# A fused two-layer encoder trunk: the first feed-forward's last down product in two passes, a Sqrt and a reciprocal for the norm behind it, and GpSimd on four rows of the final norm

## The chip, the cores and the metric

The kernel runs on one core of a Trainium2 chip. The metric is the device time of one execution in microseconds (us), the median of three timed runs. The profile comes from one further execution. TensorE (PE) does matrix products into PSUM, VectorE (DVE), ScalarE (ACT) and GpSimd (POOL) work element by element, SyncE (SP) starts DMAs. Each engine has its own instruction stream; they meet at semaphores.

## What is computed

Two streams of frames (1024 prompt frames and 64 sample frames, D = 1024) pass through two layers that share all weights:

```
for layer in range(2):
    x = x + mixer(rmsnorm(x, norm_mix[layer]))       # layer 0: RG-LRU, layer 1: RWKV-7
    x = x + conv_ffn(rmsnorm(x, norm_ffn[layer]))    # D_FF = 3072
y = rmsnorm(x, norm_final)

rmsnorm(x, g)  = x * rsqrt(mean(x*x, -1) + 1e-6) * g
conv_ffn(h)    : u = causal_dwconv(h @ w_up); g, val = split(u); (gelu(g) * val) @ w_down
rwkv7 (start)  : prev = shift(h); xx = prev - h; x_j = h + xx*mu_j for six j; then r, k, v, w, a, g from x_j
```

Recurrent states of each mixer and convolution are outputs too.

## The kernel before

**Layout.** Activations are transposed: `X` is 8 rows (row k holds channels 128k to 128k+127 on the 128 partitions) of 1092 columns (1024 prompt frames, a gap of 4, 64 sample frames). A row is cut into three column blocks of 364. `WIDE` is the first two blocks (728 columns), `LAST` the third (364). A product is in three parts (high by high, high by low, low by high) of values split in two, so each 128x128 weight block costs three matmuls per column block. `ACC[0]` is PSUM banks 0 to 2, `ACC[1]` banks 3 to 5; product m goes to `ACC[m % 2]`, signals `acc_ready`, and TensorE starts product m + 2 only when product m has been taken (`taken0`, `taken1`). Weight tiles come in by DMA to `RAW`, ScalarE makes the high part `WH` (`w_hi`), GpSimd the low part `WL` (`w_lo`).

**A feed-forward** has 12 steps of four up products and eight down products; each down product d adds to row d of `X`. VectorE takes it (`X[d] += ACC`).

**The norm behind the first feed-forward** (`norm`, L520 on ScalarE, L1321 on TensorE, `take_all` on VectorE). The last eight down products have full width (18 matmuls each). VectorE takes row d, ScalarE squares it into a scratch row, VectorE adds the squares into `T[:, 3]`. When seven squares have been added, TensorE sums over partitions with a matrix of ones (`ONES`), plain fp32 matmuls: three blocks of `T[:, 3]`, then three of the last square. ScalarE turns the sum into the factor, Ln and then Exp with scale -0.5, with a table load between. VectorE then forms row k of the RWKV input, `HF[k] = X[k] * mix1[k] * factor`, ScalarE copies it to `HS[k]`, VectorE subtracts for the low part, and TensorE begins the first two RWKV products (L1444), 36 matmuls per k. Beside the down products GpSimd prepares those products' weights: from `RAW` it forms the shift weights (L1147, L1149), waits for ScalarE's copy (`sh_hi`), and makes low parts of them (`sh_lo`) and of two weight tiles (`w_lo`); TensorE waits for both `sh_lo` and both `w_lo` before it begins L1444.

**The kernel's end** (`final_down`, `final_rows`, `final_square`, `final_root`). Here the last down product already has two passes: eight products over WIDE (12 matmuls each), then eight over LAST (6 each). After the fourth LAST product TensorE sums the WIDE squares; after the eighth, the LAST ones in two matmuls. VectorE computes `X * final * factor` row by row, eight WIDE rows (three LAST adds fall between them) and eight LAST rows, and SyncE sends each row out, all WIDE rows first.

The wait that orders VectorE's own stream: each of its instructions waits for its predecessor's semaphore (`own`).

Of the kernel before, what the change touches and what calls it, by code (L numbers as in the profile page):

```python
# [138 lines left out]
M_PROJ = M_N2 + 1  # L139
# [28 lines left out]
def build(nc, io):  # L168
    ctx = ExitStack()
    with ctx:  # L170
# [86 lines left out]
        def sum_parts(m):  # L257
# [8 lines left out]
            w_hi w_lo acc_ready taken0 taken1 pads vprep absv hist kept tap conv gelu squared primed summed normed root_ln rstd y_dve  # L266
# [12 lines left out]

        ONES, MG = CO[:, 0:P], CO[:, C_MG:C_MG + P]  # L280
# [48 lines left out]
        def _(sp):  # L329
# [156 lines left out]
            for cols in (WIDE, LAST):  # L486
                for k in range(KT):
                    sp.wait_ge(*t.next("y_dve"))
                    sp.dma_start(io["yT"][k][:, cols], X[:, k, cols]).then_inc(*t.made(f"dma_y{k % 2}"))
# [6 lines left out]
        def _(act):  # L496
# [23 lines left out]
            def norm(m, source, n=None, weights=None):  # L520

                nonlocal sums
                for k in range(KT):
                    if weights == "two" and k == KT // 2:
                        w_hi(n, m - KT // 2)
                    source(k)
                    if k >= 3:
                        act.wait_ge(*t.at("summed", sums + k - 2))
                    run(T[:, 3 if k == 0 else 4 + k % 2, 0:COLS], X[:, k, :], ACT.Square, "squared")
                sums += KT - 2  # L530
                run(DV[:, 13, 0:1], CO[:, 0:1], ACT.Ln, "primed")
                if weights == "both":
                    w_hi(n, 0)
                if weights in ("both", "two"):
                    w_hi(n + 1, m)
                evacuate(m, row3(T[:, 2, 0:COLS]), ACT.Ln, bias=RMS_EPS, scale=1.0 / D)
                run(T[:, 2, 0:COLS], T[:, 2, 0:COLS], ACT.Exp, "rstd", scale=-0.5)
# [162 lines left out]
            plus = added(m - KT)  # L700

            def added_and_shift(k):
                if k in (1, 3):
                    act.wait_ge(*t.next("mu_w"))
                    run(TR[:, 6 + k // 2, 0:D], T[:, k // 2, 0:D], ACT.Copy, "sh_hi")
                plus(k)

            norm(m, added_and_shift, n, "two")
# [332 lines left out]
            def final_square(m, k, cols, base):  # L1041

                act.wait_ge(*t.at(f"taken{m % 2}", m // 2 + 1))
                if k >= 3:
                    act.wait_ge(*t.at("summed", base + k - 2))
                run(T[:, 3 if k == 0 else 4 + k % 2, cols], X[:, k, cols], ACT.Square, "squared")

            def final_root(sums_at, out):

                act.wait_ge(*t.next("normed"))  # L1050
                run(out, sums_at, ACT.Ln, "root_ln", bias=RMS_EPS, scale=1.0 / D)
                run(out, out, ACT.Exp, "rstd", scale=-0.5)

            m -= KT
            for k in range(KT):
                final_square(m + k, k, WIDE, sums)
# [13 lines left out]
        def _(pool):  # L1070
# [206 lines left out]
            ffn()  # L1277


        @block.tensor  # L1280
        def _(pe):
# [38 lines left out]

            def norm(m):  # L1321

                if m >= 2:
                    pe.wait_ge(*t.at(f"taken{m % 2}", m // 2))
                pe.wait_ge(*t.next("summed", KT - 2))
                for j in range(CH):
                    pe.matmul(ACC[m % 2][:, j, :], ONES, T[:, 3, j * CW:(j + 1) * CW], start=True, stop=False)
                pe.wait_ge(*t.next("squared", KT))
                for j in range(CH):
                    mm = pe.matmul(ACC[m % 2][:, j, :], ONES, T[:, 5, j * CW:(j + 1) * CW], start=False, stop=True)  # L1330
                mm.then_inc(*t.made("acc_ready"))
# [51 lines left out]
            def final_down(m, n):  # L1383
# [21 lines left out]
                pe.wait_ge(*t.next("summed", KT - 2))  # L1405
# [4 lines left out]
            def ffn(m, n, final=False):  # L1410
# [336 lines left out]
            ffn(m, n, final=True)  # L1747
# [3 lines left out]
        def _(dve):  # L1751
# [72 lines left out]
            def take_all(m, last, bias=False, first=0):  # L1824
# [5 lines left out]
                if last:  # L1830
                    t.n["squared"] += 1
# [603 lines left out]
```

## Time and profile before

| | |
|---|---|
| timed runs | 3153.45 us median (3153.28 to 3154.48) |
| profiled execution, its own time | 3144.15 us |
| span of the profiled execution | 3142.3 us |
| mean granted TensorE clock, share of full | 0.986 |
| TensorE busy | 3008.6 us, 96% of the span |
| VectorE, ScalarE, GpSimd busy | 1794.4, 1022.5, 964.7 us |

The span runs from the first to the last instruction; the profiled execution's own time has 1.85 us more around it. Its time lies 9.3 us under the median of the timed runs, so durations from the trace are differences to be put on that median. A busy TensorE is not TensorE at its peak: its matmul ends are modelled. In the timelines "start us" is counted from the span's start, the second number is the duration, the bracket at the end is the engine's idle time before the instruction and what ended it; a group `xN` merges N neighbours.

### The profile page before, as it was taken

What the parts mean: (1) busy time and instruction counts of PE and PEld (TensorE: products, weight loads), DVE (VectorE), ACT (ScalarE), POOL (GpSimd) and SP (SyncE); (2) the same over time, 40 slices, a digit from 0 to 9 for tenths busy, and PEclk for the clock granted to TensorE, in tenths of its full rate; (3) what the DMA queues carried; (4) which work ended last, traced back from release to release, by engine and by line L of the source; (5) the groups of instructions that cost most, each with busy time, mean ns of one, the idle gap of its engine ahead of it and who ended that gap; (6) DMA issues with size and microseconds to landing.
All of it is one profiled execution on the core that took longest, in us unless ns stands there. A gap on an engine that the chain in (4) does not pass through costs nothing.

```text
span 3142.3 us, 66696 instructions
## 1 busy us (share of the span) xinstructions
PE 3008.6 (96%) x29230; PEld 2891.2 (92%) x29230; DVE 1794.4 (57%) x1871; ACT 1022.5 (33%) x1274; POOL 964.7 (31%) x549
## 2 busy tenths in 40 slices
PE   8999999999999998899998999998999999999997
PEld 7899999999999997889986877887999999999997
DVE  7766765555556556502206777763566555555657
ACT  6433411111111113633326777773311111111113
POOL 2222223222222323313314555552132322222231
PEclk9999999999999998999998999998999999999999
DMA  3111111111111111242231222213111111111111
GB/s 107 47 43 41 42 41 43 46 48 41 48 41 48 41 48 34 107 155 90 88 121 54 78 69 77 73 35 102 42 48 41 42 47 48 41 48 41 48 41 71
DMA packets 88684, 185.66 MB, mean 59 GB/s; under 512 B 29024, under 2 KB 53088, under 8 KB 88416
## 3 DMA queue, kind: packets, MB, share of 16 engines
q1 hardware_dynamic: 81504, 154.73, 15.7%
q10 hardware_dynamic: 6912, 26.84, 2.1%
q8 instruction: 231, 3.78, 0.5%
q14 instruction: 37, 0.30, 0.0%
HBM read 145.01 MB, written 36.53 MB: 58 GB/s over the span
## 4 chain that ended last, share of the span: by engine, by line
PE 78%; DVE 14%; ACT 5%; issue 1%; POOL 1%; DMA 0%; DVEq 0%; ACTq 0%; SPq 0%; POOLq 0%
PE PS L1294 65%; PE PS L1509 9%; DVE T L1757 3%; DVE X L1757 2%; ACT T L502 2%; PE PS L1444 2%; DVE T L1772 2%; DVE BK L1757 1%; ACT L502 1%; DVE HL L1767 1%; DVE G L1757 1%; DVE T L1767 1%; ACT UV L502 1%; PE PS L1358 1%; DVE T L1762 1%
## 5 line engine op out<-in xcount | busy, mean ns | idle before, releaser
L1077 POOL TENSOR_TENSOR WL<-RAW,WH 128x1024 fp32r<-128x1024 f32 x204 | 495.8, 2431 | 1390.9 <-ACT WH L502 1387.0
L1294 PE MATMUL PS<-HH,WH 128*128 128x364 f32 x3456 | 771.4, 331 | 32.2 <-DVE HL L1767 12.8
L1294 PE MATMUL PS<-HH,WL 128*128 128x364 f32 x3456 | 767.6, 331 | 0.0
L1294 PE MATMUL PS<-HL,WH 128*128 128x364 f32 x3456 | 764.5, 330 | 0.0
L1294 PEld LDWEIGHTS PS<-HH,WH 128*128 128x128 f32 x3456 | 600.8, 189 | 40.7 <-issue 13.6
L1294 PEld LDWEIGHTS PS<-HH,WL 128*128 128x128 f32 x3456 | 605.5, 189 | 0.0
L1294 PEld LDWEIGHTS PS<-HL,WH 128*128 128x128 f32 x3456 | 603.1, 189 | 0.0
L502 ACT ACTIVATE WH<-RAW 128x1024 fp32r<-128x1024 f32 x204 | 216.6, 1062 | 824.6 <-PE PS L1294 809.6
L1757 DVE TENSOR_TENSOR T<-PS,T 128x1092 f32<-128x1092 f32 x110 | 142.6, 1296 | 553.4 <-PE PS L1294 536.9
L1757 DVE TENSOR_TENSOR X<-PS,X 128x1092 f32<-128x1092 f32 (+2 forms) x232 | 291.5, 1257 | 231.9 <-PE PS L1294 219.6
L1294 PE MATMUL PS<-PH,WH 128*128 128x364 f32 x1296 | 289.6, 332 | 11.0 <-DVE X L1757 5.8
L1294 PE MATMUL PS<-PL,WH 128*128 128x364 f32 x1296 | 288.1, 331 | 0.0
L1294 PE MATMUL PS<-PH,WL 128*128 128x364 f32 x1296 | 287.9, 330 | 0.0
L1077 POOL TENSOR_TENSOR PL<-T,PH 128x1092 fp32r<-128x1092 f32 x56 | 142.8, 2549 | 433.9 <-ACT PH L502 433.9
L1767 DVE SCALAR_TENSOR_TENSOR T<-T,FP 128x1092 f32<-128x1092 f32 x192 | 264.4, 1377 | 6.8
L1294 PEld LDWEIGHTS PS<-PH,WH 128*128 128x128 f32 x1296 | 224.3, 189 | 20.5 <-DVE X L1757 17.4
L1294 PEld LDWEIGHTS PS<-PH,WL 128*128 128x128 f32 x1296 | 227.1, 189 | 0.0
L1294 PEld LDWEIGHTS PS<-PL,WH 128*128 128x128 f32 x1296 | 225.6, 189 | 0.0
L502 ACT ACTIVATE PH<-T 128x1092 fp32r<-128x1092 f32 x56 | 62.6, 1118 | 483.3 <-DVE T L1757 483.2
L1772 DVE COPY T<-FP 128x2 f32<-128x2 f32 x96 | 206.1, 2147 | 3.3
L502 ACT ACTIVATE T<-T 128x1092 f32<-128x1092 f32 (+2 forms) x62 | 68.4, 1103 | 307.3 <-DVE T L1767 307.1
L1757 DVE TENSOR_TENSOR T<-T 128x1092 f32<-128x1092 f32 (+2 forms) x110 | 149.4, 1359 | 15.1 <-ACT T L502 6.6
(191 smaller groups left out, 3383.8 us busy)
## 6 DMA issues: line engine op xcount, KB each, us to landing
RAW<-weights SPq DMA_DIRECT2D x204, 512.0 KB, 3.4
scratch<-T ACTq DMA_DIRECT2D x31, 546.0 KB, 3.3
scratch<-SR ACTq DMA_DIRECT2D x14, 546.0 KB, 3.0
X<-xT SPq DMA_DIRECT2D x8, 546.0 KB, 7.7
T<-scratch_m SPq DMA_DIRECT2D x8, 512.0 KB, 4.2
KK<-scratch SPq DMA_DIRECT2D x16, 192.0 KB, 2.8
LW<-scratch SPq DMA_DIRECT2D x16, 192.0 KB, 2.5
AA<-scratch SPq DMA_DIRECT2D x16, 192.0 KB, 3.3
```

The costliest lines, as they stand in the source:

```text
L502: act.activation(out, in_, func, bias=bias, scale=scale).then_inc(*t.made(event, n))
L1077: pool.tensor_tensor(out, full, hi, ALU.subtract).then_inc(*t.made(event))
L1294: mm = pe.matmul(acc[:, j, :], a, b[:, j * CW:(j + 1) * CW], start=(i == 0 and q == 0), stop=(i == len(blocks) - 1 and q == 2))
L1358: mm = pe.matmul(ACC[(m + q) % 2][:, j, :], GW[f % 2][:, q, :], U[f % 2][:, j * CW:(j + 1) * CW], start=True, stop=True)
L1444: mm = pe.matmul(acc[:, j, :], w, x[:, k, j * CW + c:(j + 1) * CW + c], start=(k == 0 and i == 0), stop=(k == KT - 1 and i == 5))
L1509: mm = pe.matmul(out, lhsT, rhs, start=first, stop=True, skip_group_check=True)
L1757: dve.tensor_tensor(out, a, b, op).then_inc(*t.made(event, n))
L1762: dve.tensor_scalar(out, a, s1, s2, op1, op2).then_inc(*t.made(event))
L1767: dve.scalar_tensor_tensor(out=out, in0=a, scalar=s, in1=b, op0=op1, op1=op2).then_inc(*t.made(event, n))
L1772: dve.tensor_copy(out, a).then_inc(*t.made(event))
```

## The change

1. The first feed-forward's last down product now has two passes as well (`two_pass_down` for both). The squares, their adds and the sums are cut into WIDE and LAST parts there too, and the function `norm` is gone. Eight product numbers more are used (`M_PROJ = M_N2 + KT`, before `+ 1`), so `ACC` banks swap roles in what follows.
2. In both places LAST squares of rows 5, 6 and 7 are no longer added by VectorE but summed by TensorE, one ones-matmul each behind that of `T[:, 3]`; VectorE adds four (rows 1 to 4). Their scratch slots (`square_at`) rotate so that ScalarE waits for fewer adds.
3. The norm behind the first feed-forward: ScalarE does Sqrt (table loaded early), WIDE and LAST apart, and VectorE takes a `reciprocal` of each part. The copies `sh_hi` move to behind squares 4 and 6, the two `w_hi` to behind the WIDE and the LAST squares. The RWKV rows are then formed whole, as before.
4. The final norm: ScalarE writes the WIDE factor into PSUM (`RSP`, banks 3 and 4) and copies it to `T[:, 2]`; it also forms `X[4+i] * final` for four rows (`weighted`). GpSimd multiplies these four rows by the factor; VectorE does the other four WIDE rows and all LAST rows and reads the factor from PSUM. SyncE sends WIDE rows in the order 0, 4, 1, 5, 2, 6, 3, 7.

```diff
-M_PROJ = M_N2 + 1
+M_PROJ = M_N2 + KT
...
+        def square_at(k):
+            c = 2 if k == 0 else (2, 0, 1)[(k - 1) // 2 % 3]
+            return T[:, 3 if k == 0 else 4 + k % 2, c * CW:(c + 1) * CW]
+        RSP = PS[:, 3:5, 0:CW]
@@ SyncE, end @@
+            for i in range(KT // 2):
+                for k, rows in ((i, "y_dve"), (KT // 2 + i, "y_pool")):
+                    sp.wait_ge(*t.next(rows))
+                    sp.dma_start(io["yT"][k][:, WIDE], X[:, k, WIDE]).then_inc(*t.made(f"dma_y{k % 2}"))
+            for k in range(KT):
+                sp.wait_ge(*t.next("y_dve"))
+                sp.dma_start(io["yT"][k][:, LAST], X[:, k, LAST]).then_inc(*t.made(f"dma_y{k % 2}"))
@@ ScalarE @@
+            def wide_square(m, k):
+                act.wait_ge(*t.at(f"taken{m % 2}", m // 2 + 1))
+                if k >= 3:
+                    act.wait_ge(*t.at("summed", sums + k - 2))
+                run(T[:, 3 if k == 0 else 4 + k % 2, WIDE], X[:, k, WIDE], ACT.Square, "squared")
+            def last_square(m, k):
+                act.wait_ge(*t.at(f"taken{m % 2}", m // 2 + 1))
+                if k >= 3:
+                    act.wait_ge(*t.at("summed", sums + (k == KT - 1)))
+                run(square_at(k), X[:, k, LAST], ACT.Square, "squared")
+            def part_root(sums_at, log, out):
+                act.wait_ge(*t.next("normed"))
+                run(log, sums_at, ACT.Ln, "root_ln", bias=RMS_EPS, scale=1.0 / D)
+                run(out, log, ACT.Exp, "rstd", scale=-0.5)
+            def weighted(i):
+                run(T[:, (0, 1, 6, 7)[i], WIDE], X[:, KT // 2 + i, WIDE], ACT.Copy, "weighted", scale=vec("final", KT // 2 + i))
...
@@ ScalarE, behind the first feed-forward @@
-            norm(m, added_and_shift, n, "two")
+            for k in range(KT):
+                wide_square(m + k, k)
+                if k in (4, 6):
+                    act.wait_ge(*t.next("mu_w"))
+                    run(TR[:, 6 + (k - 4) // 2, 0:D], T[:, (k - 4) // 2, 0:D], ACT.Copy, "sh_hi")
+            act.preload_act_table(ACT.Sqrt)
...
+            for k in range(4):
+                last_square(m + k, k)
+            act.wait_ge(*t.next("normed"))
+            run(row2(T[:, 2, WIDE]), PS[:, 6:8, 0:CW], ACT.Sqrt, "rstd", bias=RMS_EPS, scale=1.0 / D)
+            w_hi(n, m + 4)
+            for k in range(4, KT):
+                last_square(m + k, k)
+            w_hi(n + 1, m + 8)
+            act.wait_ge(*t.next("normed"))
+            run(T[:, 2, LAST], PS[:, 0, 0:CW], ACT.Sqrt, "rstd", bias=RMS_EPS, scale=1.0 / D)
@@ ScalarE, end (behind four LAST squares) @@
-            final_root(PS[:, 6:8, 0:CW], row2(T[:, 2, WIDE]))
+            weighted(0)
+            part_root(PS[:, 6:8, 0:CW], row2(T[:, 2, WIDE]), RSP)
+            run(row2(T[:, 2, WIDE]), RSP, ACT.Copy, "weighted")
             for k in range(4, KT):
-                final_square(m + k, k, LAST, sums)
+                last_square(m + k, k)
+            for i in range(1, KT // 2):
+                weighted(i)
             run(DV[:, 13, 0:1], CO[:, 0:1], ACT.Ln, "primed")
-            final_root(PS[:, 0, 0:CW], T[:, 2, LAST])
+            part_root(PS[:, 0, 0:CW], T[:, 2, LAST], PS[:, 1, 0:CW])
@@ GpSimd, end @@
+            for i in range(KT // 2):
+                pool.wait_ge(*t.at("weighted", i + 2))
+                tt(X[:, KT // 2 + i, WIDE], T[:, (0, 1, 6, 7)[i], WIDE], T[:, 2, WIDE], ALU.mult, "y_pool", own=False)
@@ TensorE, two_pass_down (both feed-forwards) @@
-                pe.wait_ge(*t.next("summed", KT - 2))
+                pe.wait_ge(*t.next("summed", 4))
                 pe.matmul(PS[:, 0, 0:CW], ONES, T[:, 3, LAST], start=True, stop=False)
-                pe.wait_ge(*t.next("squared", 2 * KT))
-                pe.matmul(PS[:, 0, 0:CW], ONES, T[:, 5, LAST], start=False, stop=True).then_inc(*t.made("normed"))
+                for k in range(5, KT):
+                    pe.wait_ge(*t.next("squared", KT + 6 if k == 5 else 1))
+                    mm = pe.matmul(PS[:, 0, 0:CW], ONES, square_at(k), start=False, stop=(k == KT - 1))
+                mm.then_inc(*t.made("normed"))
@@ VectorE: take_parts, both feed-forwards (LAST pass) @@
+                    if 3 <= d <= 6:
+                        dve.wait_ge(*t.next("squared", 2 if d == 3 else 1))
+                        tt(T[:, 3, LAST], T[:, 3, LAST], square_at(d - 2), ALU.add, "summed")
@@ VectorE, behind the first feed-forward @@
+            for cols in (WIDE, LAST):
+                dve.wait_ge(*t.next("rstd"))
+                dve.wait_ge(*t.own())
+                dve.reciprocal(T[:, 2, cols], T[:, 2, cols]).then_inc(*t.made("tap"))
@@ VectorE, end @@
+            for k in range(KT // 2):
+                stt(row2(X[:, k, WIDE]), row2(X[:, k, WIDE]), vec("final", k), RSP, ALU.mult, ALU.mult, "y_dve")
+            dve.wait_ge(*t.next("rstd"))
+            for k in range(KT):
+                stt(X[:, k, LAST], X[:, k, LAST], vec("final", k), PS[:, 1, 0:CW], ALU.mult, ALU.mult, "y_dve")
```

## Rows read from the trace of the kernel before

**Rows 1.** The page of the profile: busy time by engine

```profile
PE 3008.6 (96%) x29230; PEld 2891.2 (92%) x29230; DVE 1794.4 (57%) x1871; ACT 1022.5 (33%) x1274; POOL 964.7 (31%) x549
```

**Rows 2.** The chain in order of time, 1205 to 1320 us: start us, us, what

```profile
1235.19 3.98 PE PS L1327 x6
1239.17 2.46 PE PS L1330 x6
...
1242.75 1.28 ACT L502
...
1248.17 51.02 PE PS L1444 x288
...
1299.66 12.25 PE PS L1294 x72
```

**Rows 3.** Timeline of VectorE, first norm: start, us, instruction, idle and releaser

```profile
1208.16 1.30 DVE L1757 TENSOR_TENSOR X<-PS,X 128x1092 f32<-128x1092 f32 x1 [1.71 <-PE PS L1294]
...
1215.89 3.34 DVE L1757 TENSOR_TENSOR T<-T 128x1092 f32<-128x1092 f32 x1 [0.41 <-ACT T L502]
...
1224.13 1.91 DVE L1757 TENSOR_TENSOR T<-T 128x1092 f32<-128x1092 f32 x1
1226.15 1.30 DVE L1757 TENSOR_TENSOR X<-PS,X 128x1092 f32<-128x1092 f32 x1
...
1232.35 1.30 DVE L1757 TENSOR_TENSOR X<-PS,X 128x1092 f32<-128x1092 f32 x1
```

**Rows 4.** Timeline of GpSimd over the same stretch

```profile
1211.15 2.41 POOL L1149 TENSOR_TENSOR RAW<-RAW,T 128x1024 f32<-128x1024 f32 x1
1213.70 1.90 POOL L1147 TENSOR_TENSOR T<-RAW,V 128x1024 f32<-128x1024 f32 x1
1215.68 2.40 POOL L1149 TENSOR_TENSOR RAW<-RAW,T 128x1024 f32<-128x1024 f32 x1
1218.22 6.67 POOL L1077 TENSOR_TENSOR TR<-T,TR 128x1024 fp32r<-128x1024 f32 x2
1225.03 3.26 POOL L1077 TENSOR_TENSOR WL<-RAW,WH 128x1024 fp32r<-128x1024 f32 x1
1237.55 2.35 POOL L1077 TENSOR_TENSOR WL<-RAW,WH 128x1024 fp32r<-128x1024 f32 x1 [9.26 <-ACT WH L502]
```

**Rows 5.** Forms, 3095 to 3143 us: busy us, mean ns, idle before

```profile
L1767 DVE SCALAR_TENSOR_TENSOR X<-X,V,T 128x728 f32<-128x728 f32 x8 | 7.8, 977 | 0.4
...
L502 ACT ACTIVATE T<-X 128x728 f32<-128x728 f32 x8 | 6.5, 816 | 10.3 <-DVE X L1757 10.3
L1757 DVE TENSOR_TENSOR T<-T 128x728 f32<-128x728 f32 x7 | 6.4, 918 | 0.7
...
L1767 DVE SCALAR_TENSOR_TENSOR X<-X,V,T 128x364 f32<-128x364 f32 x8 | 4.8, 598 | 0.4
L1757 DVE TENSOR_TENSOR X<-PS,X 128x364 f32<-128x364 f32 x8 | 4.3, 537 | 2.4 <-PE PS L1396 1.8
```

**Rows 6.** Forms of VectorE in the first 60 us

```profile
L1767 DVE SCALAR_TENSOR_TENSOR DV<-DV 128x8 f32<-128x8 f32 x8 | 1.3, 167 | 0.3
...
L1772 DVE COPY T<-V 128x1 f32<-128x1 f32 x6 | 0.9, 153 | 0.2
...
L1841 DVE RECIPROCAL DV<-DV 128x8 f32<-128x8 f32 x1 | 0.2, 203 | 0.0
```

**Rows 7.** Timeline of TensorE at the kernel's end

```profile
3118.59 1.39 PE L1403 MATMUL PS<-T,CO 128*128 128x364 f32 x4
...
3128.83 1.58 PE L1406 MATMUL PS<-T,CO 128*128 128x364 f32 x2 [4.67 <-DVE T L1757]
```

**Rows 8.** Timeline of VectorE at the kernel's end

```profile
3128.81 11.17 DVE L1767 SCALAR_TENSOR_TENSOR X<-X,V,T 128x728 f32<-128x728 f32 x14
```

**Rows 9.** Timeline of ScalarE at the kernel's end

```profile
3133.45 0.51 ACT L502 ACTIVATE T<-T 128x364 f32<-128x364 f32 x1
```

**Rows 10.** Stretches: us, busy us of PE, PEld, DVE, ACT, POOL, PEclk (granted clock), DMA, GB/s

```profile
1235.00:1239.00 4.00, 3.81 (x7) 2.23 (x8) 0.05 (x1) 2.35 (x3) 1.45 (x1) 0.50 0.00 0
```

More of the change, by code:

```diff
@@ L265, in build @@
             dma_y0 dma_y1 dma_st
-            w_hi w_lo acc_ready taken0 taken1 pads vprep absv hist kept tap conv gelu squared primed summed normed root_ln rstd y_dve
+            w_hi w_lo acc_ready taken0 taken1 pads vprep absv hist kept tap conv gelu squared primed summed normed root_ln rstd weighted y_dve y_pool
             h_full h_hi h_lo h_lo1 h_used mixhalf hf p_full p_hi p_lo tan root post
@@ L518, in _ @@
             sums = 0
[L520 to L537, printed above, removed]
+            def wide_square(m, k):
[14 more added lines that the diff above has]
+                run(T[:, (0, 1, 6, 7)[i], WIDE], X[:, KT // 2 + i, WIDE], ACT.Copy, "weighted", scale=vec("final", KT // 2 + i))
             def scaled_hi(k, name):
@@ L1039, in _ @@
             assert (m, n) == (M_N4, N_TILES)
[L1041 to L1052, printed above, removed]
             m -= KT
             for k in range(KT):
-                final_square(m + k, k, WIDE, sums)
+                wide_square(m + k, k)
             run(DV[:, 13, 0:1], CO[:, 0:1], ACT.Ln, "primed")
@@ L1422, in ffn @@
                 m, n = down(m, n, STEPS - 2)
-                if final:
-                    return final_down(m, n)
-                return down(m, n, STEPS - 1)
+                return two_pass_down(m, n)
             m, n = ffn(m, n)
-            norm(m)
-            m += 1
             for q in range(2):
@@ L1746, in _ @@
                 m, n = m + 1, n + 1
-            ffn(m, n, final=True)
+            ffn(m, n)
         @block.vector
@@ L1822, in take, with take_rest @@
                     stt(x, ACC[m % 2], bias, x, ALU.add, ALU.add, f"taken{m % 2}", m // 2 + 1)
-            def take_all(m, last, bias=False, first=0):
-                for d in range(first, KT):
-                    take(m + d, d, vec("b_out", d) if bias else None)
-                    if last and d >= 2:
-                        add_squares(d - 1)
-                if last:
-                    t.n["squared"] += 1
+            def take_rest(m):
+                for d in range(3, KT):
+                    take(m + d, d)
             dve.wait_ge(*t.at("dma_vec", 1))
@@ L1979, in _, with take_parts @@
             fill(T[:, 0:2, 0:PAD], 0.0, "pads")
[L1981 to L1990 removed]
+            def take_parts(m):
                 for d in range(KT):
@@ L2002, in final_rows, with wide_added, ffn @@
                     if d == 0:
-                        added_to(KT - 1, WIDE)
-                    if 3 <= d <= 5:
-                        added_to(d - 2, LAST)
-                dve.wait_ge(*t.next("rstd"))
-                for k in range(2):
-                    final(k, WIDE)
-                for k in range(4, KT - 1):
-                    added_to(k, LAST)
-                for k in range(2, KT):
-                    final(k, WIDE)
-                dve.wait_ge(*t.next("rstd"))
-                for k in range(KT):
-                    final(k, LAST)
-            def ffn(m, stored, final=False):
+                        wide_added(KT - 1)
+                    if 3 <= d <= 6:
+                        dve.wait_ge(*t.next("squared", 2 if d == 3 else 1))
+                        tt(T[:, 3, LAST], T[:, 3, LAST], square_at(d - 2), ALU.add, "summed")
+                t.n["squared"] += 3
+            def wide_added(k):
+                dve.wait_ge(*t.next("squared", 2 if k == 1 else 1))
+                tt(T[:, 3, WIDE], T[:, 3, WIDE], T[:, 4 + k % 2, WIDE], ALU.add, "summed")
+            def ffn(m, stored):
                 def step(s, m):
@@ L2058, in ffn @@
                 m = step(STEPS - 1, m)
-                take_all(m, False, first=3)
+                take_rest(m)
                 m += KT
-                if final:
-                    return final_rows(m)
-                take_all(m, True)
-                return m + KT
+                take_parts(m)
+                return m + 2 * KT
             m = ffn(m, 0)
```

52 lines of the change are left out of this document (13 added, 39 removed).

## The prediction

> **What bounds the kernel.** I read the page first: TensorE is busy for 96% of the span and every other engine for at most 57% [rows 1]. So a change elsewhere counts only where TensorE waits for it. The change touches two such places. The chain in order of time shows the first: from the last take of the first feed-forward (VectorE, begun at 1232.35, 1.30 long, so 1233.65 [rows 3]) it runs through one add, the ones-matmuls at 1235.19 (3.98 and 2.46 us), ScalarE's Ln, a table load of 1.28 and Exp, the first RWKV row, and reaches TensorE again at 1248.17 [rows 2]. From there it lies on TensorE alone, 51.02 us for 288 matmuls and then 12.25 for 72: whatever moves the start at 1248.17 moves all that follows by as much. The distance from last take to restart is 14.5 us. The second place is the end, where VectorE works to 3139.98 (14 final rows in 11.17 us from 3128.81 [rows 8]) and only the last output DMA follows.
>
> **Prices.** All for blocks of 728 and 364 columns [rows 5]: WIDE take or add 0.92, with the gap to the next 1.02; LAST take or add 0.54, with gap 0.64; a WIDE square 0.82, a LAST one 0.51 [rows 5, 9]. A down matmul costs 12.25 / 72 = 0.17 [rows 2], so a WIDE product (12) 2.0 and a LAST one (6) 1.0. A ones-matmul over 364 columns shows as two passes; at the full clock four took 1.39, so 0.62 a matmul, but after a wait of 4.67 us two passes took 1.58, so some 1.25 a matmul [rows 7]. The windows show 0.50 for the granted clock in 1235 to 1239, that is 1.2 instead of 2.4 GHz, behind TensorE's wait there [rows 10].
>
> **A lock between VectorE and GpSimd.** An add of squares begun at 1215.89 took 3.34 us, not 1.30, and ended at 1219.23; GpSimd's instruction of 1215.68 ended at 1218.08, 1.15 earlier [rows 3, 4]. The add at 1224.13 (1.91) ends 1.15 behind GpSimd's pair (1218.22 + 6.67 = 1224.89), and GpSimd's next, begun 1225.03 during the add, ends at 1228.29, 2.25 behind it. Yet the take at 1226.15, in the middle of that, has its 1.30: it reads PSUM and one row of SBUF. So an instruction of VectorE with two SBUF inputs and one of GpSimd exclude each other for their whole length; I take 0.77 behind the holder for a WIDE add (0.92 less the same 0.15), 0.39 for a LAST one. In the kernel before this cost little, for takes come every 2.98 us and a pair of take and add needs 2.8. In two passes a WIDE product comes every 2.0 us and take and add need 2.04: VectorE has no slack left, and each block is handed on to TensorE, which may be only two products ahead.
>
> **First norm, walked.** The first full take is at 1208.16; a WIDE product has six matmuls fewer, so take 0 is at 1207.1, take 1 at 1209.1, take 2 at 1211.1. GpSimd, as before, holds the port from 1211.15 with its first subtraction (2.41), then has the 1.90 product and the second subtraction (2.40) [rows 4]. Add 1 waits for the first: ends 1214.3. Take 3 1215.3; add 2 waits for the product (now 1216.1): 1216.8; take 4 1217.9; add 3 waits for the second subtraction (1219.1): 1219.9; take 5 1220.9; add 4 waits for the first low part of the shift weights (from 1219.95, 2.4): 1223.1; take 6 1224.1, add 5 1225.2, take 7 1226.2; ScalarE's second `sh_hi` now lies behind square 6, so GpSimd's second low part begins just then and add 6 ends at 1229.4. Without the lock it would be 1223.4 or so: six us of it are the lock. LAST takes 0 to 3 end at 1230.1, 1231.7, 1232.4, 1233.5 with the last WIDE add between. TensorE does LAST 3 by 1232.8, the WIDE sums by 1234.05, LAST 4 to 7 by 1238.05. But Sqrt and `w_hi` follow on ScalarE (to 1236.1), GpSimd's `w_lo` then holds the port to 1238.7, and LAST add 3 stands in front of takes 6 and 7 on VectorE: add 3 1239.1, take 6 1239.7, add 4 1240.4, take 7 1241.0. That is **7.35 us later** than 1233.65.
>
> **Behind the last take.** Square 7 to 1241.6, the fourth ones-matmul to 1243.0 (three are done by then at the full clock), Sqrt of LAST to 1243.6. Meanwhile VectorE takes the reciprocal of WIDE. The trace has only one reciprocal, of 8 elements: 203 ns against 167 for a two-input instruction of 8 [rows 6]. If that is a fixed cost, the two cost 0.95 and 0.58. If it is per element, it is 4.5 ns above the 1.04 of an ordinary one, 5.5 ns, so 4.2 and 2.2 us. An upper end is (203 - 153) / 8 = 6.25 ns, from a copy of one element: 4.7 and 2.4. I take 5.5: 36 ns more for eight elements is much for a fixed cost when other kinds stand within a few ns of each other. So WIDE 1241.15 to 1245.35, LAST to 1247.6, row 0 (1.36) to 1249.05, then as before 1.48 from there to TensorE: **1250.5**. From last take to restart 9.5 instead of 14.5. The ones-matmuls in two groups of three (6.4 us) and Ln, load, Exp (3.5) are gone for it. Sum: +7.35 - 5.0 = **+2.3 us**. The low part of the second tile (1242.85 to 1245.25) is hidden by the reciprocals.
>
> The Trainium skill ("SBUF — State Buffer", Who interferes with whom) states the same exclusive lock, and that it is taken only where VectorE has two SBUF inputs; the trace agrees (1.30 for the take, 3.34 for the add), and it is this that speaks against two passes here; by rule and by rows the six us of the walk are the same. The Trainium skill ("ScalarE: Activation LUTs", What ACT_TABLE_LOAD costs) puts a switch at 1283 ns and a drain of about 1380; by it the removed load would give 1.4 us more, but here the load of 1.28 is followed by Exp at once, so the trace decides.
>
> Bank parity (8 product numbers for 1) exchanges two equal accumulators: nothing, as each product waits for the take two before it in both. Costs at the restart are the same: TensorE was at half clock behind its wait before and will be again.
>
> **The end, walked.** WIDE pass unchanged. On ScalarE, from the fourth LAST square (about 3120.0): `weighted` 0.9, Ln 0.8, load 1.28, Exp 0.8, the copy 0.8, four squares 2.3, three `weighted` 2.8, load and primer 1.5, Ln, load, Exp 2.4: 3134.1 with gaps. LAST add 4 waits for square 4 and then for GpSimd's first final row (about 1.7 for 728 columns, from 2.40 for 1024 [rows 4]), and take 7 and square 7 stand behind it: +0.9. So the LAST factor comes at 3135.0 (before 3133.96 [rows 9]). VectorE's LAST rows began at 3128.81 + 6 x 1.03 = 3134.9 and now begin at 3135.0, eight at 0.65 [rows 5]: 3140.2. The four WIDE rows taken from VectorE (4.1 us) lie in its new wait for the factor: nothing gained. GpSimd's four end by 3134.5, and the outputs' queue is emptier than before: **+0.1**. Bounds: -0.8 if add 4 does not wait, +1.5 if a row with a PSUM factor costs 0.2 more.
>
> **Sum.** Profiled execution 3144.15 + 2.4 = 3146.6; on the median of the timed runs 3153.45 + 2.4 = **3155.9 us**. The measurement can tell about 0.2%, 6.3 us, from no change.
>
> **Rivals.** (a) The reciprocal is cheap. LAST is ready at 1244.2, but row 0 has two SBUF inputs and waits for `w_lo` until 1245.25: restart 1247.9, -0.3, total 3153.3. For it: one number of 8 elements proves little. Chance 0.2. (b) The port is mostly free: GpSimd's work falls into gaps, or VectorE wins the lock. Then take 7 is near the end stage's own (last take about 26 us behind the pass's start) at 1233.5, restart 1243.0 with the dear reciprocal, -5.2, 3148.4; with the cheap one 1240.0, -8.2, 3145.4. Against it: GpSimd is busy without pause from 1208.9 to 1218 here, and was not at the end. Chance 0.15. (c) The other side: the clock. The walk has TensorE waiting 1.3, 1.0 and 2.9 us between 1223 and 1230. If the granted clock falls there, LAST 2 to 7 cost 2.0 each and the sums double: TensorE ends at 1245.4, take 7 at 1246.2, restart 1255.7: +7.5, 3161.0. It decides from a fall before about 1231; later, it is hidden behind the reciprocal of WIDE. For it: 0.50 behind 4.4 us of waiting [rows 10]; against: each wait is shorter and work lies between. Chance 0.08. (d) The reciprocal is dearer still: 6.25 ns an element and ones-matmuls at half clock give restart 1251.5, +3.3, 3156.9. Chance 0.12. The Trainium skill ("VectorE: DVE Perf Modes", Walkthrough) speaks of a repeat count of 8 for it; read as 8 cycles an element it gives an estimate of 9.4 us for both parts instead of 6.4, restart 1253.5, +5.3; no row shows it.
>
> The forecast keeps 0.45. Beyond 6.3 us on the fast side lies only the better half of (b) and what errors of the walk add, 0.1; on the slow side (c) and a corner of (d), 0.1; within, 0.8. The range 3148.0 to 3160.5 leaves out the cheap case of (b) and (c).
>
> **What would show it.** Adds `T<-T` of 728 columns over 1.3 us between 1211 and 1230, VectorE without gaps there while TensorE waits for its takes; the last LAST take at 1241; RECIPROCAL 4.2 and 2.2 us; the first L1444 matmul near 1250.5. At the end: a wait of VectorE of 3 to 4 us before eight LAST rows, last one ended at 3140 plus the shift. It is wrong if reciprocals take under 1 us and the port is free (restart before 1243), or if the granted clock shows 0.5 before the last LAST product.

## The result and the profile after

Eleven timed runs of the changed kernel gave a median of 3154.42 us (3148.9 to 3160.04), eleven of the kernel before 3151.62 us. The ratio is **1.0017, 95% interval 1.0010 to 1.0025**: about 5.4 us slower (3.2 to 7.9), where 2.4 were forecast. The ratio is not the quotient of the two medians: these lie 2.8 us apart, the two means 4.3. All of them say slower, and none fixes the size to better than a few us. The profiled execution took 3150.86 us (before 3144.15). First its page, span and busy time by engine:

```profile
span 3149.1 us, 66744 instructions
...
PE 3005.4 (95%) x29234; PEld 2888.5 (92%) x29234; DVE 1803.2 (57%) x1880; ACT 1027.9 (33%) x1286; POOL 970.7 (31%) x553
```

TensorE has no more to do than before [rows 1]; it waits longer. The timeline of VectorE at the first norm (start us, duration, instruction, idle before it and releaser):

```profile
1207.38 0.92 DVE L1762 TENSOR_TENSOR X<-PS,X 128x728 f32<-128x728 f32 x1 [0.69 <-PE PS L1403]
...
1212.37 2.22 DVE L1762 TENSOR_TENSOR T<-T 128x728 f32<-128x728 f32 x1
...
1215.72 1.41 DVE L1762 TENSOR_TENSOR T<-T 128x728 f32<-128x728 f32 x1
...
1218.26 1.90 DVE L1762 TENSOR_TENSOR T<-T 128x728 f32<-128x728 f32 x1
...
1221.28 2.11 DVE L1762 TENSOR_TENSOR T<-T 128x728 f32<-128x728 f32 x1
...
1226.56 3.07 DVE L1762 TENSOR_TENSOR T<-T 128x728 f32<-128x728 f32 x1
...
1238.43 1.90 DVE L1762 TENSOR_TENSOR T<-T 128x364 f32<-128x364 f32 x1
...
1241.72 0.54 DVE L1762 TENSOR_TENSOR X<-PS,X 128x364 f32<-128x364 f32 x1
...
1242.50 7.24 DVE L2056 RECIPROCAL T<-T 128x728 f32<-128x728 f32 x2
1249.77 1.36 DVE L1772 SCALAR_TENSOR_TENSOR HF<-X,V,T 128x1092 f32<-128x1092 f32 x1
```

and of GpSimd beside it:

```profile
1211.41 2.41 POOL L1165 TENSOR_TENSOR RAW<-RAW,T 128x1024 f32<-128x1024 f32 x1
1213.97 2.39 POOL L1163 TENSOR_TENSOR T<-RAW,V 128x1024 f32<-128x1024 f32 x1
1216.43 2.95 POOL L1165 TENSOR_TENSOR RAW<-RAW,T 128x1024 f32<-128x1024 f32 x1
1220.23 2.39 POOL L1093 TENSOR_TENSOR TR<-T,TR 128x1024 fp32r<-128x1024 f32 x1 [0.85 <-ACT TR L511]
1226.49 2.36 POOL L1093 TENSOR_TENSOR TR<-T,TR 128x1024 fp32r<-128x1024 f32 x1 [3.87 <-ACT TR L511]
1237.54 2.40 POOL L1093 TENSOR_TENSOR WL<-RAW,WH 128x1024 fp32r<-128x1024 f32 x1 [8.69 <-ACT WH L511]
```

These lines show the lock: five of the seven WIDE adds take 2.22, 1.41, 1.90, 2.11 and 3.07 us instead of 0.92, and each of these ends 0.77 or 0.78 us behind the end of a GpSimd instruction (1211.41 + 2.41 = 1213.82 and 1214.59; 1226.49 + 2.36 = 1228.85 and 1229.63; likewise the 364-column add of 1238.43, which ends 0.39 behind `w_lo`). The two adds that met no GpSimd instruction, and all WIDE takes, keep their 0.92. The last take ends at 1242.26, then two reciprocals run for 7.24 us, and the first RWKV row starts at 1249.77.

The chain in order of time behind that (start us, us, what; "issue" is time for which the profile names no wait), then ScalarE's timeline at the end of the first RWKV products, after and before:

```profile
1252.61 50.89 PE PS L1449 x288
1303.49 1.75 issue
1305.25 12.26 PE PS L1313 x72
```

```profile
1301.67 1.28 ACT L511 ACT_TABLE_LOAD   x1
1302.97 2.18 ACT L511 ACTIVATE T<-PS 64x1092 f32<-64x1092 f32 x2
```

```profile
1296.23 1.12 ACT L502 ACTIVATE HH<-T 128x1092 fp32r<-128x1092 f32 x1 [1.94 <-PE PS L1444]
1297.38 2.18 ACT L502 ACTIVATE T<-PS 64x1092 f32<-64x1092 f32 x2
```

TensorE restarts at 1252.61, 4.4 us later than before [rows 2]. It then stands for 1.75 us before the first W_r product (L1313 here, the first product behind the two LoRA products), where before it stood 1299.66 - 1299.19 = 0.47 [rows 2]. ScalarE shows why: a table load of 1.28 us now stands before the Tanh of the LoRA product (in the pair at 1302.97). Before, the same pair at 1297.38 followed at once: the table loaded for Exp was still there, and it serves Tanh too.

The granted clock in two stretches of the changed kernel (us, busy us of PE, PEld, DVE, ACT, POOL, PEclk, DMA share, GB/s):

```profile
1229.00:1233.00 4.00, 2.68 (x9) 2.38 (x10) 3.16 (x5) 1.25 (x3) 0.00 (x0) 0.72 0.00 0
...
1241.00:1245.00 4.00, 2.71 (x8) 1.44 (x8) 3.65 (x4) 2.54 (x4) 0.96 (x1) 1.00 0.37 127
```

Two numbers matter here. The granted clock did dip while LAST products 2 and 3 ran: behind a wait of TensorE of 2.54 us it was 0.50 from about 1231 to 1234, which gives 0.72 over the first stretch. And it was at 1.00 for the ones-matmuls around the last take, unlike before [rows 10].

The end of the kernel, VectorE and GpSimd:

```profile
3105.61 0.92 DVE L1762 TENSOR_TENSOR X<-PS,X 128x728 f32<-128x728 f32 x1 [0.69 <-PE PS L1403]
...
3131.86 1.54 DVE L1762 TENSOR_TENSOR T<-T 128x364 f32<-128x364 f32 x1 [1.12 <-ACT T L511]
...
3134.15 4.00 DVE L1772 SCALAR_TENSOR_TENSOR X<-X,V,PS 128x728 f32<-128x728 f32 x4
3141.30 5.00 DVE L1772 SCALAR_TENSOR_TENSOR X<-X,V,PS 128x364 f32<-128x364 f32 x8 [3.15 <-ACT PS L511]
```

```profile
3131.28 1.73 POOL L1191 TENSOR_TENSOR X<-T 128x728 f32<-128x728 f32 x1 [24.06 <-ACT T L511]
3135.60 5.08 POOL L1191 TENSOR_TENSOR X<-T 128x728 f32<-128x728 f32 x3 [2.59 <-ACT T L511]
```

VectorE has four WIDE rows (4.00 us), then waits 3.15 us for the LAST factor, then does eight LAST rows: it ends at 3146.30, 40.69 us behind the first WIDE take at 3105.61. Before, this was 40.99 (3139.98 behind a take at 3098.99). The lock shows here as well: the LAST add of 3131.86 takes 1.54 instead of 0.54 and ends 0.39 us behind GpSimd's first row. The outputs' rate in 40 equal slices, before (3115 to 3145 us) and after (3120 to 3150 us):

```profile
GB/s 0 0 0 0 0 0 0 0 0 0 11 0 0 0 0 163 357 400 74 0 50 415 322 369 361 381 369 361 367 334 375 286 303 311 311 56 0 0 0 0
```

```profile
GB/s 0 0 0 0 0 0 0 0 0 0 0 0 0 0 0 0 0 0 0 0 0 272 396 373 412 384 373 412 373 373 373 353 355 388 381 363 351 33 0 0
```

The change starts the outputs later but then keeps the queue full to the end, at 351 to 412 GB/s, where before the last slices had 286 to 311. The span ends 2.80 us behind VectorE's last row, before 2.32 (3142.3 - 3139.98). Sum of the end: -0.30 + 0.48 = +0.2 us.

### The profile page after: what moved, and what is told of

The parts are those of the page before. It is cut to its first block, busy times and chain, and to the rows that moved or that the text cites. A ratio compares the mean times of both kernels' runs of the same rounds, so it can differ in the third digit from the quotient of the medians.

```text
span 3149.1 us, 66744 instructions
## 1 busy us (share of the span) xinstructions
PE 3005.4 (95%) x29234; PEld 2888.5 (92%) x29234; DVE 1803.2 (57%) x1880; ACT 1027.9 (33%) x1286; POOL 970.7 (31%) x553
## 4 chain that ended last, share of the span: by engine, by line
PE 77%; DVE 14%; ACT 6%; issue 1%; POOL 1%; DMA 0%; DVEq 0%; ACTq 0%; SPq 0%; POOLq 0%
PE PS L1313 64%; PE PS L1514 9%; DVE T L1762 3%; DVE X L1762 2%; ACT T L511 2%; DVE T L1777 2%; PE PS L1449 2%; ACT L511 1%; DVE BK L1762 1%; DVE HL L1772 1%; DVE G L1762 1%; DVE T L1772 1%; ACT UV L511 1%; PE PS L1403 1%; PE PS L1365 1%
## 5 line engine op out<-in xcount | busy, mean ns | idle before, releaser
L1313 PE MATMUL PS<-HH,WH 128*128 128x364 f32 x3456 | 771.2, 331 | 33.0 <-DVE HL L1772 12.6
L1313 PE MATMUL PS<-HH,WL 128*128 128x364 f32 x3456 | 767.7, 330 | 0.0
L1313 PE MATMUL PS<-HL,WH 128*128 128x364 f32 x3456 | 764.0, 329 | 0.0
L1313 PEld LDWEIGHTS PS<-HH,WH 128*128 128x128 f32 x3456 | 601.0, 189 | 41.3 <-issue 14.7
L1313 PEld LDWEIGHTS PS<-HH,WL 128*128 128x128 f32 x3456 | 606.1, 189 | 0.0
L1313 PEld LDWEIGHTS PS<-HL,WH 128*128 128x128 f32 x3456 | 602.7, 189 | 0.0
L1313 PE MATMUL PS<-PH,WH 128*128 128x364 f32 x1248 | 278.3, 331 | 10.3 <-DVE X L1762 5.2
L1313 PE MATMUL PS<-PH,WL 128*128 128x364 f32 x1248 | 277.4, 330 | 0.0
L1313 PE MATMUL PS<-PL,WH 128*128 128x364 f32 x1248 | 277.3, 330 | 0.0
L1313 PEld LDWEIGHTS PS<-PH,WH 128*128 128x128 f32 x1248 | 216.1, 189 | 18.8 <-DVE X L1762 15.7
L1313 PEld LDWEIGHTS PS<-PH,WL 128*128 128x128 f32 x1248 | 218.8, 189 | 0.0
L1313 PEld LDWEIGHTS PS<-PL,WH 128*128 128x128 f32 x1248 | 217.0, 189 | 0.0
L511 ACT ACTIVATE T<-T 128x1092 f32<-128x1092 f32 x59 | 66.0, 1119 | 307.5 <-DVE T L1772 307.4
```

The costliest lines, as they stand in the source:

```text
L511: act.activation(out, in_, func, bias=bias, scale=scale).then_inc(*t.made(event, n))
L1313: mm = pe.matmul(acc[:, j, :], a, b[:, j * CW:(j + 1) * CW], start=(i == 0 and q == 0), stop=(i == len(blocks) - 1 and q == 2))
```

## Experiments

Executions differ by several us in places that the change doesn't touch (see below), so besides the ratios I compare distances inside one execution. Zero is the start of the last take before the last down product (1205.15 in before, 1205.40 in after). The numbers are differences of times in the timelines. Their scatter has to be kept in mind: e4_tail_only has the first norm of the kernel before, unchanged, and its restart and W_r product differ from before by 0.23 and 0.34 us.

| kernel | last take ends | TensorE restarts | first W_r product | ratio to before, 95% interval |
|---|---|---|---|---|
| before | 28.50 | 43.02 | 94.51 | |
| after | 36.86 | 47.21 | 99.85 | 1.0017 (1.0010 to 1.0025) |
| e1_ln_exp | 37.51 | 45.98 | 96.24 | 1.0005 (0.9996 to 1.0013) |
| e2_preload | 36.81 | 47.15 | 98.50 | 1.0007 (0.9999 to 1.0016) |
| e3_port_free | 29.76 | 40.12 | 92.68 | single execution |
| e4_tail_only | 28.52 | 43.25 | 94.85 | 0.9994 (0.9985 to 1.0003) |
| e5_three_groups | 28.51 | 39.56 | 91.11 | 0.9982 (0.9973 to 0.9990) |
| e6_three_groups_tail | 28.50 | 39.54 | 89.81 | 0.9984 (0.9975 to 0.9992) |
| e7_recip_one_pass | 28.51 | 47.77 | 100.22 | single execution |

The ratios of e1, e2 and e4 to e6 are against runs of the kernel before made beside them; none was measured against the changed kernel itself. So that e1 and e2 are faster than the change rests on the distances, not on times.

**e1_ln_exp: Ln and Exp in two parts in place of Sqrt and the reciprocals.**

```diff
-            run(row2(T[:, 2, WIDE]), PS[:, 6:8, 0:CW], ACT.Sqrt, "rstd", bias=RMS_EPS, scale=1.0 / D)
+            part_root(PS[:, 6:8, 0:CW], row2(T[:, 2, WIDE]), row2(T[:, 2, WIDE]))
...
-            run(T[:, 2, LAST], PS[:, 0, 0:CW], ACT.Sqrt, "rstd", bias=RMS_EPS, scale=1.0 / D)
+            part_root(PS[:, 0, 0:CW], T[:, 2, LAST], T[:, 2, LAST])
...
-                dve.reciprocal(T[:, 2, cols], T[:, 2, cols]).then_inc(*t.made("tap"))
```

Ahead of each part ScalarE also runs one small Ln, which brings the load of its table forward (not shown).

> The changed kernel with Ln and Exp (in two parts) in the first norm instead of Sqrt and the two reciprocals. Theory A (what the change loses lies in three terms at the first norm: the port lock in two passes, 7.2 us of reciprocals behind the last take, and one more table load before Tanh, because Sqrt's table does not hold Tanh and Exp's does): the reciprocals' 7.2 us go, Ln, load and Exp of the LAST part (2.3 us) come back, and ScalarE's longer WIDE part makes the last take up to 1.5 us later; TensorE restarts 1 to 2 us earlier than in the changed kernel (45.2 us behind the first WIDE take there), and the load before Tanh is gone, 1.3 us more by the first W_r product. All in all 2 to 4 us faster than the change, still 2 to 3 us slower than before. Theory B (the reciprocals are hidden behind other work and the loss is elsewhere): no change at the restart.

TensorE's timeline (restart, and first W_r product):

```profile
1252.66 1.25 PE L1448 MATMUL PS<-HS,WH 128*128 128x364 f32 x3 [6.35 <-ACT HS L511]
...
1302.92 0.77 PE L1312 MATMUL PS<-HH,WH 128*128 128x364 f32 x3 [0.47 <-POOL WL L1092]
```

and ScalarE behind the last LAST take, which ends at 1244.19:

```profile
1244.74 1.28 ACT L511 ACT_TABLE_LOAD   x1
...
1247.99 1.28 ACT L511 ACT_TABLE_LOAD   x1
1249.29 0.51 ACT L511 ACTIVATE T<-T 128x364 f32<-128x364 f32 x1
```

The restart comes 1.2 us earlier than in the changed kernel. So the reciprocals were on the chain, though only 1.2 of their 7.2 us come back: the last take is 0.65 later, and behind the last square two table loads, `w_hi` (1.06), Ln and the LAST Exp now stand on ScalarE one behind the other, until 1249.80. The first W_r product comes 3.6 us earlier: 1.2 from the restart, 1.3 because its gap is back at 0.47, and 1.1 because TensorE's clock came back sooner. Between three and five us behind the restart the granted clock was 1.00 in e1 (first line) and 0.50 in the changed kernel (second):

```profile
1255.66:1257.66 2.00, 2.00 (x14) 2.00 (x13) 1.82 (x4) 1.12 (x1) 0.00 (x0) 1.00 0.00 0
```

```profile
1255.61:1257.61 2.00, 2.00 (x9) 2.00 (x8) 1.83 (x4) 1.12 (x1) 0.00 (x0) 0.50 0.00 0
```

That last part need not be the edit's: e5 and e6 below differ in the same way with the same first norm. The expectation of 2 to 4 us against the change was met by the distance, 2.5 us without the clock's share. It expected 2 to 3 us slower than before; the W_r product is 1.7 later, and the medians say 1.5 (3151.0 us of 12 runs, before 3149.48), with an interval that includes no change.

**e2_preload: the table that Tanh needs, loaded while ScalarE waits.**

```diff
             run(T[:, 2, LAST], PS[:, 0, 0:CW], ACT.Sqrt, "rstd", bias=RMS_EPS, scale=1.0 / D)
+            act.preload_act_table(ACT.Sigmoid)
```

> The changed kernel with Sigmoid's table loaded right behind the last Sqrt, while ScalarE waits for the reciprocals. Theory A: the table holds Tanh too, so the loads before Tanh and before Sigmoid at the end of the first RWKV products are gone; the gap of TensorE before the first W_r product goes from 1.75 us back to about 0.47: 1.3 us faster than the change, restart unchanged. Theory B (that gap is no table load but bank order, since 8 product numbers more swap the accumulators): the gap stays at 1.75.

```profile
1252.22 1.25 PE L1450 MATMUL PS<-HS,WH 128*128 128x364 f32 x3 [8.22 <-ACT HS L511]
...
1303.57 0.73 PE L1314 MATMUL PS<-HH,WH 128*128 128x364 f32 x3 [0.47 <-issue]
```

The gap is 0.47 again and the restart unchanged, with the accumulators still swapped: for this gap bank order is out, the load it was. The time (ratio 1.0007) is not clear of no change.

**e3_port_free: GpSimd reads nothing while VectorE adds.** Left out: the shift weights, so the two LoRA products are not those of the reference.

```diff
-                    pool.tensor_tensor(by_mu(T[:, q, 0:D])[:, :, a:z], RAW[q][:, :, a:z], mu, ALU.mult).then_inc(*t.made("mu_part"))
+                    pool.memset(by_mu(T[:, q, 0:D])[:, :, a:z], 0.0).then_inc(*t.made("mu_part"))
-                pool.tensor_tensor(RAW[q][:, :, :], RAW[q][:, :, :], by_mu(T[:, q, 0:D]), ALU.subtract).then_inc(*t.made("mu_w"))
+                pool.memset(RAW[q][:, 0:1, 0:1], 0.0).then_inc(*t.made("mu_w"))
-                rest(TR[:, q, 0:D], T[:, q, 0:D], TR[:, 6 + q, 0:D], "sh_hi", "sh_lo")
+                pool.wait_ge(*t.next("sh_hi"))
+                pool.wait_ge(*t.own())
+                pool.memset(TR[:, q, 0:D].bitcast(F32), 0.0).then_inc(*t.made("sh_lo"))
```

> The changed kernel in which GpSimd does not form the shift weights: its products and subtractions there are fills, which read nothing from SBUF (the two LoRA products are then wrong). Theory A (the lock on the shared read port delays VectorE's adds by some 8 us): WIDE adds take 0.92 us each, the last LAST take ends some 27 to 28 us behind the first WIDE take instead of 34.9, and TensorE restarts 6 to 8 us earlier. Theory B (two passes are slow on VectorE by themselves, 2.04 us for take and add against 2.0 for a product): the last take moves by less than 2 us.

VectorE and GpSimd:

```profile
1206.46 0.92 DVE L1764 TENSOR_TENSOR X<-PS,X 128x728 f32<-128x728 f32 x1 [0.69 <-PE PS L1405]
...
1211.45 0.92 DVE L1764 TENSOR_TENSOR T<-T 128x728 f32<-128x728 f32 x1
...
1221.66 0.92 DVE L1764 TENSOR_TENSOR T<-T 128x728 f32<-128x728 f32 x1
...
1230.41 1.90 DVE L1764 TENSOR_TENSOR T<-T 128x364 f32<-128x364 f32 x1
...
1233.69 0.54 DVE L1764 TENSOR_TENSOR X<-PS,X 128x364 f32<-128x364 f32 x1
```

```profile
1211.39 0.95 POOL L1163 MEMSET T<- 128x1024 f32 x1 [1.91 <-DMA RAW<-weights]
...
1221.58 0.95 POOL L1169 MEMSET TR<- 128x1024 f32 x1 [3.13 <-ACT TR L511]
1229.51 2.40 POOL L1093 TENSOR_TENSOR WL<-RAW,WH 128x1024 fp32r<-128x1024 f32 x1 [6.98 <-ACT WH L511]
```

Every WIDE add has 0.92 us (the fills at 1211.39 and 1221.58 ran at the same time as the adds of 1211.45 and 1221.66 and held neither up). The one GpSimd instruction with two inputs that is left, `w_lo` at 1229.51, still holds the LAST add of 1230.41 (1.90, ended 0.40 behind it). The last LAST take ends 27.8 us behind the first WIDE take instead of 34.9, and the restart is 7.1 us earlier. Of the 7.1 us, 6.1 are there at the end of the sixth WIDE add (18.1 us behind the zero instead of 24.2); the other 1.0 comes with the clock, which stayed at 1.00 through the LAST products here, for TensorE no longer waited 2.54 us before them. So the delay of the takes is the lock and what follows from it. And without it the changed kernel restarts 2.9 us earlier than the kernel before (40.12 against 43.02).

**e4_tail_only: the kernel before with the change's end alone.**

```diff
-M_PROJ = M_N2 + KT
+M_PROJ = M_N2 + 1
...
+            m, n = ffn(m, n)
+            norm(m)
+            m += 1
```

(the first feed-forward and its norm as before on all engines; the end as in the change)

> The kernel before with only the change at the end: LAST squares 5 to 7 on TensorE, four WIDE rows on GpSimd, the factor read from PSUM. Theory A (all of the loss is at the first norm): within 1 us of before, VectorE's last row ends 40.7 us behind the first WIDE take of the last pass (before 41.0). Theory B (half of the loss is at the end or in the output queue): 2 us or more slower than before.

Median 3149.27 us of 11 runs against 3149.48: ratio 0.9994 (0.9985 to 1.0003). VectorE's last row ends 40.68 us behind the first WIDE take, the span 2.75 behind that, together 0.1 us more than before. No loss shows at the end; the interval alone would leave room for 0.9 us of loss there and 4.7 of gain.

**e5_three_groups: the kernel before, one pass, fewer adds and earlier ones-matmuls.**

```diff
-                pe.wait_ge(*t.next("summed", KT - 2))
+                pe.wait_ge(*t.next("summed", KT - 3))
                 for j in range(CH):
                     pe.matmul(ACC[m % 2][:, j, :], ONES, T[:, 3, j * CW:(j + 1) * CW], start=True, stop=False)
-                pe.wait_ge(*t.next("squared", KT))
-                for j in range(CH):
-                    mm = pe.matmul(ACC[m % 2][:, j, :], ONES, T[:, 5, j * CW:(j + 1) * CW], start=False, stop=True)
+                for r in (4, 5):
+                    pe.wait_ge(*t.next("squared", KT - 1 if r == 4 else 1))
+                    for j in range(CH):
+                        mm = pe.matmul(ACC[m % 2][:, j, :], ONES, T[:, r, j * CW:(j + 1) * CW], start=False, stop=(r == 5))
...
-                    if last and d >= 2:
+                    if last and 2 <= d < KT - 1:
                         add_squares(d - 1)
```

> The kernel before, one pass, with the ones-matmuls of the first norm in three groups (the sum of squares 0 to 5, square 6, square 7), so that VectorE's last two adds go and only the last group stands behind the last take. Theory A (the chain from last take to restart is what counts): before, an add of 1.3 and six ones-matmuls at half the granted clock (6.4 us) stand there; now a square of 1.1 and three ones-matmuls of 0.62 (full clock) to 1.25 (half clock). Restart 3 to 5 us earlier, 38 to 40 us behind the last take of the product before, against 43.0; all in all 3 to 5 us faster than before (ratio about 0.9987). Theory B (TensorE's clock or the start of the RWKV products takes the gain back): restart earlier, but the first W_r product at its old 94.5 us.

The edit takes one add away, not two: VectorE has six adds of squares in this norm before, five here. The sums start 2.8 us earlier against the zero (27.26 us behind it for 30.04).

TensorE's timeline, and its granted clock in one stretch:

```profile
1233.33 2.07 PE L1327 MATMUL PS<-T,CO 128*128 128x364 f32 x6 [1.65 <-DVE T L1758]
1235.24 3.83 PE L1331 MATMUL PS<-T,CO 128*128 128x364 f32 x12
1245.63 1.25 PE L1445 MATMUL PS<-HS,WH 128*128 128x364 f32 x3 [6.55 <-ACT HS L502]
```

```profile
1235.00:1239.00 4.00, 4.00 (x14) 2.22 (x12) 0.00 (x0) 3.27 (x4) 0.51 (x1) 1.00 0.00 0
```

The first group begins behind a wait of 1.65 us instead of 4.42, while the clock is still full, and it stays so: 12 passes take 3.83 us where before the first six alone took 3.98 [rows 2]. The restart is 3.5 us earlier and the W_r product 3.4. Median 3143.63 us of 11 runs against 3149.04: **ratio 0.9982 (0.9973 to 0.9990)**, 5.7 us with an interval of 3.1 to 8.5. It beats the kernel before, and by the two intervals the changed one too.

**e6_three_groups_tail: the same with the change's end.**

> The same together with the change's end. Theory A: the end is worth 0 (its VectorE work ends 0.3 us earlier, its output queue is 0.5 us longer), so the same 3 to 5 us as with the old end. Theory B (the end gains or costs by itself): differs from that by more than 2 us.

3144.5 us, ratio 0.9984 (0.9975 to 0.9992): the same within the intervals. No gain of the end shows here either.

**e7_recip_one_pass: the kernel before with Sqrt and one reciprocal.**

```diff
-                run(DV[:, 13, 0:1], CO[:, 0:1], ACT.Ln, "primed")
+                act.preload_act_table(ACT.Sqrt)
...
-                evacuate(m, row3(T[:, 2, 0:COLS]), ACT.Ln, bias=RMS_EPS, scale=1.0 / D)
-                run(T[:, 2, 0:COLS], T[:, 2, 0:COLS], ACT.Exp, "rstd", scale=-0.5)
+                evacuate(m, row3(T[:, 2, 0:COLS]), ACT.Sqrt, bias=RMS_EPS, scale=1.0 / D)
...
+            dve.reciprocal(T[:, 2, 0:COLS], T[:, 2, 0:COLS]).then_inc(*t.made("tap"))
```

> The kernel before, one pass, with Sqrt and one reciprocal of 1092 columns in the first norm. Theory A (6.46 ns an element): the reciprocal takes 7.1 us, Exp and its table load (2.4 us) go: restart 4.7 us later than before (47.7 us behind the last take of the product before), and 1.3 us more by the first W_r product through the load before Tanh. Theory B (the reciprocals cost nothing in the change because they lie beside the LAST sum): says nothing of one pass; with it alone the loss of two passes would be all 4.2 us and the reciprocal's price irrelevant.

```profile
1242.86 6.98 DVE L2075 RECIPROCAL T<-T 128x1092 f32<-128x1092 f32 x1 [7.87 <-ACT T L502]
```

The reciprocal takes 6.98 us for 1092 columns, 6.4 ns each; the restart is 4.75 us later than before and the W_r product 5.7. Sqrt and reciprocal alone, without the two passes, lose as much at the restart as the whole change: 4.75 us there, 4.2 here. In two passes the last take comes 8.4 us later, but the way from it to the restart is 10.4 us instead of 19.3, for the sums are earlier, at full clock, and beside the reciprocals. Four traces make a table of the restart, in us behind the zero:

| | Ln and Exp | Sqrt and reciprocal |
|---|---|---|
| one pass | 43.02 (before) | 47.77 (e7) |
| two passes | 45.98 (e1) | 47.21 (change) |

Each of the two edits alone makes the restart later, and the losses do not add up, because in two passes the reciprocals lie beside other work.

**e8_late_weighted: ScalarE's three later operands for GpSimd behind the LAST factor (on e6).**

```diff
-            for i in range(1, KT // 2):
-                weighted(i)
             run(DV[:, 13, 0:1], CO[:, 0:1], ACT.Ln, "primed")
             part_root(PS[:, 0, 0:CW], T[:, 2, LAST], PS[:, 1, 0:CW])
+            for i in range(1, KT // 2):
+                weighted(i)
```

> Three ones groups and the change's end, but ScalarE makes the three later GpSimd operands behind the LAST factor instead of in front of it. Theory A (the four rows given to GpSimd gain nothing because VectorE only waits longer for the LAST factor, and behind it the output queue is full): VectorE's wait of 3.15 us before its LAST rows nearly goes and its last row ends 2.8 us earlier (37.9 instead of 40.7 us behind the first WIDE take), but the outputs, issued in order behind GpSimd's later rows, end no earlier: the time from VectorE's last row to the end of the span grows from 2.7 to 5 us or more. Theory B (VectorE's end sets the span's end): that time stays at 2.7 and the end comes 2.8 us earlier.

VectorE, and SyncE's queue:

```profile
3137.72 5.00 DVE L1798 SCALAR_TENSOR_TENSOR X<-X,V,PS 128x364 f32<-128x364 f32 x8 [1.99 <-ACT PS L511]
```

```profile
3132.73 11.42 SPq L495 DMA_DIRECT2D yT<-X  x8
3144.19 4.52 SPq L498 DMA_DIRECT2D yT<-X  x8
```

VectorE ends 39.5 us behind the first WIDE take (3103.19), 1.1 us earlier than in e6 and not 2.8, for now ScalarE waits for the ones-matmuls of the LAST squares. But SyncE sends the rows in order: its eight WIDE issues last until 3144.15 because they wait for GpSimd's rows, the LAST rows go out behind them, and the span ends 8.8 us behind VectorE's last row instead of 2.7. This order costs 4.9 us at the end (from the first WIDE take to the end of the span 48.3 against 43.4), in one execution of each.

## Why the prediction was right, and where it was off

**Right: the mechanism and its place.** The walk of the lock gave adds ending at 1214.3, 1216.8, 1219.9, 1223.1 and 1229.4; the trace has 1214.6, 1217.1, 1220.2, 1223.4 and 1229.6. The last take was forecast at 1241.0 and came at 1242.3 (36.86 behind the zero where the walk had 35.85). e3 showed the lock by taking it away, and its 6.1 us at the sixth add are the "six us" of the walk. Rival (b), a port that is mostly free, is out. The end was costed at +0.1; e4 and the two traces give 0.1 to 0.2. Bank parity was costed at nothing; e2 shows it at the W_r gap only, and no run isolates it elsewhere.

**Two terms too small and one missing, all the same way.** The total by the traces is 5.34 us at the W_r product (99.85 - 94.51) and 0.2 at the end, 5.5. That lies inside the interval of the ratio (3.2 to 7.9); its nearness to the ratio's 5.4 proves little, since the medians give 2.8. Forecast was 2.4. The difference of 3.1:
- The last take, +1.0: the clock dipped during LAST 2 and 3, rival (c) in a small form (0.50 for some three us, not to the end). One of the prediction's own signs of being wrong, a clock of 0.5 before the last LAST product, did show; it cost 1.0 us and not the 5 of the rival, for the clock was back at full from about 1234. The WIDE sums, Sqrt and `w_hi` behind it came later by as much, and `w_lo` then held the port until 1239.94 and not 1238.7.
- The reciprocals, 7.15 us of work (4.71 and 2.44 on the chain) for 6.4. These are the 4.7 and 2.4 that the prediction gave as its upper end: 6.25 ns an element. The three lengths measured bear it out: 2.44, 4.71 and 6.98 us for 364, 728 and 1092 columns are 6.24 ns for each further column and some 0.17 us besides. So the copy of one element was the right thing to compare with, 5.5 ns the wrong choice of the two, and rival (d) had the right price (without its half clock, for the ones-matmuls ran at 1.00). The ones-matmuls and the LAST Sqrt were hidden behind the first reciprocal, as forecast. Rival (a), a cheap reciprocal, is out.
- **The table load before Tanh, +1.15 at the W_r product: missed altogether.** The gap grew by 1.28; the RWKV products before it were 0.13 shorter. (Gaps of 0.1 and 0.1 at the end make up the 3.1.) I wrote "whatever moves the start at 1248.17 moves all that follows by as much". That step failed: the change also took Exp's table away from ScalarE, and the next function, some 57 us behind the last Sqrt, needed a load on the chain. e1 and e2 both bring the 0.47 us gap back. The Trainium skill ("ScalarE: Activation LUTs", Table sets: the hidden batching unit) lists Tanh with the sets of Exp and of Sigmoid, names no other function in Sqrt's, and advises to batch by set; the traces agree: no load before Tanh behind Exp, one behind Sqrt, and none in e2 behind Sigmoid's table. The removed load was counted, the new one wasn't.

**Where luck came in.** The forecast of 3155.9 us lies 1.5 above the median of 3154.42, closer than its terms deserve. It started from a median of three runs, 3153.45, and the eleven have 3151.62: that error of 1.8 us covers part of the terms that were too small.

**Open.** Single executions of one kernel differ by up to 12 us. In the ten traces the way from the first W_r product to the first WIDE take of the kernel's end, whose work none of the edits changes, takes 1796.9 to 1806.3 us. Between the two profiled executions it grew by 1.0 us (1799.3 and 1800.4), which I take for this scatter. The four kernels with swapped accumulators have 1796.9 to 1802.2, the six others 1799.3 to 1806.3: no loss through bank parity shows, but one trace each cannot exclude a small effect.

## What to carry to other kernels

Before cutting a product into passes, look at who shares VectorE's second SBUF read: its take-and-add pair had 0.2 us of slack per product in one pass and none in two, and then every GpSimd instruction that reads SBUF is felt. When a function is exchanged on ScalarE, follow its table forward to the next function that needs one, however far. In a norm's tail it paid most to begin the ones-matmuls with what is already there, while TensorE's clock is still full (e5, ratio 0.9982).

## What the runs showed that I had not expected

A reciprocal on VectorE takes 6.98 us for 1092 columns where an add takes 1.30, five times as long. A GpSimd fill of 1024 columns (0.95 us) held up no add of VectorE, where a GpSimd instruction that reads did. And the slow stretch of TensorE's clock behind its wait is not the same each time: e5 and e6 restart alike, but one reached the W_r product 51.55 us later and the other 50.27; the granted clock was 0.50 for the first three us behind the restart in e6, as in e1, and for some five in e5, before and the change. What decides between the two, no run shows.
